# A second plain pair of chunks, and another order of units, in the two feed-forward stages of an encoder layer

## The reference

```python
x = layer_norm(ALPHA * x + 0.5 * swiglu(x, ffn1...), ...)
x = layer_norm(ALPHA * x + hybrid_mixer(x, ...), ...)
x = layer_norm(ALPHA * x + memory_cross_attention(x, mem, ...), ...)
x = layer_norm(ALPHA * x + 0.5 * swiglu(x, ffn2...), ...)

def swiglu(x, w_gate, w_up, w_down):      # 1024 -> 2816 -> 1024
    return (silu(x @ w_gate) * (x @ w_up)) @ w_down
```

## Time and profile before

| | us |
|---|---|
| median of three runs (1238.31 to 1239.45) | 1238.95 |
| the profiled execution, its own time | 1240.66 |
| its span, first to last instruction | 1238.9 |
| TensorE busy in the span | 1190.8 |
| VectorE, ScalarE, POOL busy | 940.2, 624.1, 257.3 |

### The profile page before, as it was taken

The page is one execution under the profiler, slowest core; times in us unless marked ns, Lnnn a source line. Parts: engine busy times, 40 slices in busy tenths (PEclk is TensorE's granted clock), DMA queues, the critical chain, the costliest instruction groups (busy, mean ns, idle before and its releaser), DMA issues.

```text
span 1238.9 us, 18583 instructions
## 1 busy us (share of the span) xinstructions
PE 1190.8 (96%) x7307; PEld 1067.7 (86%) x7307; DVE 940.2 (76%) x1221; ACT 624.1 (50%) x955; POOL 257.3 (21%) x208
## 2 busy tenths in 40 slices
PE   8699999999999999999999999999969999999996
PEld 7689999999989888878888888888969989898995
DVE  5778888888868767777764577555887898978786
ACT  3654545454536767567642225341365454545453
POOL 3232323232102200111010020001332233332301
PEclk9899999999999999999999999999989999999999
DMA  8866877777846414222273516213665778786841
GB/s 262 249 152 177 197 195 182 206 182 211 198 138 207 141 45 108 72 60 68 69 221 102 170 34 188 80 39 119 186 146 120 217 166 221 153 235 140 239 120 68
DMA packets 140646, 188.42 MB, mean 152 GB/s; under 512 B 6528, under 2 KB 106896, under 8 KB 139536
## 3 DMA queue, kind: packets, MB, share of 16 engines
q1 hardware_dynamic: 121104, 126.92, 32.9%
q0 software_dynamic: 19248, 60.30, 23.4%
q10 hardware_dynamic: 208, 0.01, 0.0%
HBM read 137.93 MB, written 7.34 MB: 117 GB/s over the span
## 4 chain that ended last, share of the span: by engine, by line
PE 80%; DVE 12%; issue 4%; ACT 3%; DMA 1%; SPq 0%; DVEq 0%; ACTq 0%
PE bank L1085 16%; PE bank L1004 11%; PE banks_scores L1085 11%; PE bank L1006 11%; PE bank L1005 11%; DVE ring_lo L2089 5%; PE bank L1011 5%; PE banks_scores L1011 3%; PE banks_scores L1004 2%; PE banks_scores L1005 2%; PE banks_scores L1006 2%; DVE x_sum L2179 2%; ACT ring_hi L1628 2%; DVE op_lo L2089 1%; PE bank L1355 1%
## 5 line engine op out<-in xcount | busy, mean ns | idle before, releaser
L2089 DVE TENSOR_TENSOR ring_lo<-raw,ring_hi 128x1024 fp32r<-128x1024 f32 x191 | 245.7, 1290 | 95.8 <-ACT ring_hi L1628 95.3
L1628 ACT ACTIVATE ring_hi<-raw 128x1024 fp32r<-128x1024 f32 x191 | 200.7, 1056 | 93.0 <-PE bank L1006 33.2
L1085 PE MATMUL bank<-xT_hi,ring_hi 128*128 128x256 f32 x480 | 137.3, 286 | 7.3 <-DVE hf L2170 5.0
L1085 PE MATMUL bank<-xT_hi,ring_lo 128*128 128x256 f32 x480 | 137.3, 286 | 0.0
L1085 PE MATMUL bank<-xT_lo,ring_hi 128*128 128x256 f32 x480 | 137.2, 286 | 0.0
L1004 PE MATMUL bank<-xT_hi,ring_hi 128*128 128x512 f32 (+1 forms) x360 | 136.6, 379 | 0.3 <-DVE gate L2746 0.3
L1006 PE MATMUL bank<-xT_hi,ring_lo 128*128 128x512 f32 (+1 forms) x360 | 134.5, 374 | 0.0
L1005 PE MATMUL bank<-xT_lo,ring_hi 128*128 128x512 f32 (+1 forms) x360 | 134.3, 373 | 0.0
L1085 PE MATMUL banks_scores<-x_s,ring_hi 128*128 128x256 f32 x640 | 117.4, 284 | 6.9 <-DVE ring_lo L2089 6.9
L1085 PEld LDWEIGHTS banks_scores<-x_s,ring_hi 128*128 128x128 f32 x640 | 100.6, 192 | 11.1 <-DVE ring_lo L2089 10.1
L1085 PEld LDWEIGHTS bank<-xT_hi,ring_hi 128*128 128x128 f32 x480 | 93.3, 194 | 9.4 <-issue 8.0
(11 more groups left out here) (421 smaller groups left out, 3164.4 us busy)
## 6 DMA issues: line engine op xcount, KB each, us to landing
raw<-in_ffn_w_gate SPq DMA_DIRECT2D x44, 512.0 KB, 4.0
raw<-in_ffn_w_up SPq DMA_DIRECT2D x44, 512.0 KB, 5.6
wd<-in_ffn_w_down SPq DMA_DIRECT2D x20, 1024.0 KB, 5.1
raw<-in_mix_w_in SPq DMA_DIRECT2D x34, 512.0 KB, 3.8
t<-in_ffn_w_down SPq DMA_DIRECT2D x20, 512.0 KB, 7.3
raw<-raw POOLq DMA_DIRECT2D x20, 512.0 KB, 4.7
raw<-gate_t POOLq DMA_DIRECT2D x20, 512.0 KB, 5.6
t<-wd POOLq DMA_DIRECT2D x10, 512.0 KB, 6.7
```

The source lines that it names most:

```text
L1085: mm = pe.matmul(dst, a[:, k, cols], b[:, k, :], start=fresh, stop=True, skip_group_check=True)
L1628: nc.scalar.activation(dst, src, copy).then_inc(unit_hi, 1)
L2089: nc.vector.tensor_tensor(dst, src, hi.bitcast(F32), ALU.subtract).then_inc(done, 1)
```

## The change

The plain units become eight, so that the first two pairs are plain and groups run from 2 to 10 (`FIRST` is 2). The two further chunks use banks 0 to 3 again: chunk 2 waits for `hidden(0)`, chunk 3 for `hidden(1)`. The x sums and their halves move behind the hidden rows of the plain chunks, and have the same order in both stages. The units of quad 0 move from group 1 and 2 to groups 2 and 3. In every group pair the down units 1 and 4, and 5 and 2, stand together behind product 5. At the end down unit 5 goes ahead of the first four end tiles and down unit 6 behind them, and tiles 4 and 7 change places; `end_low(1)` moves behind the first four tiles, `add_product` of unit 5 ahead of them. The buffer `squares_1` moves to where gate_t1 lay.

```diff
-PLAIN = 4
+PLAIN = 8
+FIRST = PLAIN // 4
...
-    order += G(1, 0, 1, 4, 3, 5) + D(0, 0) + G(1, 2, 6)
     for d in range(1, QUADS):
         a, b, done = 2 * d, 2 * d + 1, d - 1
-        order += G(a, 0, 1) + (D(done, 0) if d > 1 else [])
-        order += G(a, 4, 3) + D(done, 1) + G(a, 5) + D(done, 4) + G(a, 2, 6) + D(done, 3)
-        order += G(b, 0, 1, 4, 3) + D(done, 5) + G(b, 5) + D(done, 2) + G(b, 2, 6) + D(done, 6)
+        order += G(a, 0, 1) + D(done, 0) + G(a, 4, 3, 5) + D(done, 1, 4) + G(a, 2, 6) + D(done, 3)
+        order += G(b, 0, 1, 4, 3, 5) + D(done, 5, 2) + G(b, 2, 6) + D(done, 6)
     a, done = GROUPS, QUADS - 1
-    order += G(a, 0, 1) + D(done, 0) + G(a, 4, 3) + D(done, 1) + G(a, 5) + D(done, 4) + G(a, 2) + D(done, 3) + G(a, 6)
+    order += G(a, 0, 1) + D(done, 0) + G(a, 4, 3, 5) + D(done, 1, 4) + G(a, 2) + D(done, 3) + G(a, 6)
...
-TILE_ORDER = (0, 1, 2, 3, 5, 7, 4, 6)
+TILE_ORDER = (0, 1, 2, 3, 5, 4, 7, 6)
...
-                for m in range(2):
+                for m in range(PLAIN // 2):
...
             def weight_sums(f):
 
-                gate_sums(f, 2)
-                gate_sum_21(f, 2)
...
-            gate_sums(0, 1)
+            gate_sums(0, FIRST)
             pool.wait_ge(xt_lo, T_X1)
...
-            gate_sum_21(0, 1)
             down_sums_0(0)
+            gate_sum_21(0, FIRST)
             weight_sums(0)
...
-                def gate_up(side, n):
+                def gate_up(side, n, chunk):
                     for m in range(2):
                         ready(n + m)
+                        if m == 0 and chunk >= 2:
+                            pe.wait_ge(h_full, hidden_count(f, 0) + chunk - 1)
                         project(n + m, bank(2 * side + m))
...
                 first_units() if f == 0 else first_units_2()
+                for chunk in (2, 3):
+                    gate_up(chunk % 2, n0 + 2 * chunk, chunk)
                 for kind, g, q in SEQUENCE:
...
                     elif kind == "D":
+                        down_quad_product(g, q)
                         if (g, q) == (QUADS - 1, 5):
                             for j in TILE_ORDER[:4]:
                                 end_tile(j)
-                        down_quad_product(g, q)
-                        if (g, q) == (QUADS - 1, 5):
-                            for j in TILE_ORDER[4:6]:
-                                end_tile(j)
-                for j in TILE_ORDER[6:]:
+                for j in TILE_ORDER[4:]:
                     end_tile(j)
...
                 prep(n0 + 4)
-                x_high(3)
                 prep(n0 + 5)
-                x_high(4)
                 silu(0)
...
                 prep(n0 + 6)
-                scale_block(0)
+                x_high(3)
                 prep(n0 + 7)
-                scale_block(1)
-                if f == 0:
-                    x_high(2)
                 silu(1)
                 prep(n0 + 8)
+                x_high(4)
+                scale_block(0)
+                silu(2)
+                prep(n0 + 9)
+                scale_block(1)
+                prep(n0 + 10)
+                x_high(2)
+                part_high(0, 0)
+                silu(3)
+                prep(n0 + 11)
+                scale_block(2)
+                prep(n0 + 12)
+                scale_block(3)
...
+                    add_product(QUADS - 1, 5)
                     end_tile(0)
-                    end_low(1)
                     end_tile(1)
                     mean(0, end_mean)
                     end_tile(2)
                     end_tile(3)
                     mean(1, end_mean)
-                    add_product(QUADS - 1, 5)
+                    end_low(1)
                     first_block()
                     end_tile(5)
-                    end_tile(7)
                     gain(3, x, 1)
                     end_tile(4)
                     centre(2)
+                    end_tile(7)
                     end_tile(6)
...
                 split(n0 + 4)
-                x_first_sum()
                 split(n0 + 5)
-                x_second_sum()
                 hidden(0)
...
                 split(n0 + 6)
+                x_first_sum()
+                split(n0 + 7)
+                hidden(1)
+                x_second_sum()
+                split(n0 + 8)
                 x_low(4)
-                split(n0 + 7)
                 x_low(3)
-                if f == 0:
-                    x_fourth_sum()
-                hidden(1)
-                split(n0 + 8)
+                split(n0 + 9)
+                hidden(2)
+                x_fourth_sum()
+                split(n0 + 10)
+                x_low(2)
+                split(n0 + 11)
+                part_low(0, 0)
+                hidden(3)
+                split(n0 + 12)
                 x_third_sum()
...
                         elif q == 1:
                             part_sum_4(d)
                             if d == 0:
+                                x_low(5)
                                 part_low(0, 1)
...
                         elif q == 6 and d == QUADS - 1:
+                            end_low(0)
                             part_low(d, 6)
-                            end_low(0)
```

More of the change, by code:

```diff
@@ L178, in raw_tables @@
         keys = [(ffn_unit(f, "P", 0, j), ffn_unit(f, "P", 0, j)) for j in range(PLAIN)]
-        keys += [((f, g, b), ffn_unit(f, "G", g, q)) for g in range(1, GROUPS + 1) for b, q in BLOCKS.items()]
+        keys += [((f, g, b), ffn_unit(f, "G", g, q)) for g in range(FIRST, GROUPS + 1) for b, q in BLOCKS.items()]
         keys += [(ffn_unit(f, "L", 0, r), ffn_unit(f, "L", 0, r)) for r in range(2)]
@@ L375, in program @@
         gate = place("gate", [P, 2, SEQ], F32, z_gate)
-        squares_1 = place("squares_1", [P, 2, D], BF16, z_gate)
+        squares_1 = place("squares_1", [P, 2, D], BF16, z_q)
         c_hi = place("c_hi", [P, SEQ], BF16, z_p + 4096)
@@ L549, in group_no @@
         def group_no(f, g):
-            return GROUPS * f + g - 1
+            return (GROUPS + 1 - FIRST) * f + g - FIRST
         def hidden_count(f, g):
@@ L699, in ffn_units @@
                 for name in BLOCKS:
-                    block(1, name)
+                    block(FIRST, name)
                 if f == 0:
@@ L709, in ffn_units @@
                 down_rows(1, 0)
-                for name in BLOCKS:
-                    block(2, name)
                 for d in range(1, QUADS):
@@ L980, in _ @@
             pool.wait_ge(om_full, KC)
-            gate_sums(1, 1)
-            gate_sum_21(1, 1)
+            gate_sums(1, FIRST)
             down_sums_0(1)
+            gate_sum_21(1, FIRST)
             weight_sums(1)
@@ L1052, in corners_free @@
                     if q == 0:
[L1053 removed]
+                        pe.wait_ge(*((silu_done, hidden_count(f, g - 2) + 2) if g > FIRST + 1 else (h_full, hidden_count(f, 1) + 1)))
                     elif q == 1:
[L1055 removed]
+                        pe.wait_ge(*((corner, k - 2) if g > FIRST else (h_full, hidden_count(f, 1) + 2)))
                     elif q == 4:
                         pe.wait_ge(snap, k + 1)
[L1058 removed]
+                        pe.wait_ge(x_sum_lo, 4 * f + X_LOWS[q])
                     elif q == 3:
[L1060 removed]
+                        if g > FIRST:
                             pe.wait_ge(corner, k)
[L1062 removed]
+                        pe.wait_ge(x_sum_lo, 4 * f + X_LOWS[q])
                     elif q == 5:
                         pe.wait_ge(snap, k + 2)
[L1065 removed]
+                        pe.wait_ge(x_sum_lo, 4 * f + X_LOWS[q])
                     elif q == 2:
                         pe.wait_ge(corner, k + 2)
[L1068 removed]
+                        pe.wait_ge(x_sum_lo, 4 * f + X_LOWS[q])
                     elif q == 6:
@@ L1759, in ffn @@
                         silu_first(g)
-                    if g == 1 and kind == "G":
-                        if q in (1, 4):
-                            scale_block(2 + (q == 4))
-                        elif q == 0:
+                    if kind == "G" and g % 2 == 0:
+                        d = g // 2 - 1
+                        if (g, q) == (FIRST, 0):
+                            part_high(0, 1)
                             x_high(5)
-                            part_high(0, 0)
-                        elif q == 3 and f == 1:
-                            x_high(2)
-                        elif q == 6:
-                            part_high(0, 1)
-                    elif kind == "G" and g % 2 == 0:
-                        d = g // 2 - 1
-                        if q == 1:
+                        elif q == 1:
                             part_high(d, 4)
@@ L2368, in centre_first @@
                                                        op0=ALU.add, op1=ALU.mult).then_inc(gained, 1)
+                    add_product(QUADS - 1, 5)
                     end_tile(0)
-                    end_low(1)
                     end_tile(1)
                     mean(0, first_mean)
```

(16 more changed lines are left out.)

48 lines of the change are left out of this document (14 added, 34 removed).

## The result

The changed kernel takes 1201.08 us (median of 4 runs, 1200.91 to 1201.29) against 1239.2 for the kernel before beside it: a ratio of 0.9692, 95% interval 0.9675 to 0.9709. It is faster, as forecast, by 38.1 us; the forecast of 1198.7 is 2.4 us too low, and its range of 1195 to 1211 holds the time. The profiled execution took 1201.12 us, its span is 1199.2.

A forecast was written before the change was run, and what follows sets the result against it. TensorE, busy 96% of the span, was taken as the bound, with its few standing places. Savings of 15.2 + 12.6 + 8.2 + 4.3 = 40.3 us took the profiled 1240.66 to 1200.4, median forecast 1198.7, range 1195 to 1211.

The forecast's parts named there:

- Part 1: Both stage starts: keeping the second pair plain adds 3.7 us of TensorE work but removes standing, saving 15.2 and 12.6.
- start of stage 1: From the plain pair's end to group 2, 39.93 us becomes 24.77 if nothing stands: 15.2 saved.
- start of stage 2: From the plain pair's end to group 2, 37.41 us less 24.77: 12.6 saved.
- eight quad stands: TensorE's 1.02 us stand before product 2, eight times alike, goes whole: 8.2 us, other bound 0.
- nothing stands: Both starts: hidden rows, x sums and product 5's low half come in time, the last with 2.3 us to spare.
- Part 2: Per quad, two down units between the corner's copy and product 2 give the corner 5.5 us instead of 2.75; saves 8.2.
- Part 3, stage 1: End of stage 1: D5 ahead of the first four tiles, D6 earlier; the third memory-key unit's wait of 1.0 goes.
- Part 3, stage 2: Kernel's end: VectorE no longer stands for tile 4, with one more eviction ahead of the last; 1.7 us saved.
- The rival of the late low half: Product 5's low half lengthened by POOL's gate add: up to 1.5 us a stage, 1201.7 us; chance 0.15.
- quad stand: Rival: waits before product 2 stay because VectorE is too far behind; all eight give 1206.9 us; chance 0.12, whole or part.
- moved start wait: Rival: hidden rows late ahead of product 1 in both stages, 16.8 us, so 1215.5; chance 0.06.
- products 5 not held by the corner's copy: Denies the slower rival: ScalarE's corner copy outlasts product 3 in 18 groups; 1242 us if 5.3 behind product 4; chance 0.03.

The follow-up runs named there:

- e3: Kernel before, first x sum steps, their copies and low halves moved behind the first hidden rows, still one plain pair: 1236.26 us against 1238.66, ratio 0.9975.
- e2: Changed kernel with the first five x sum steps and their two high copies put back ahead of the first chunk's hidden rows: 1210.97 us.
- e4: Kernel before, TensorE's order kept, VectorE's split at D1 and D5 moved behind the corner subtraction: 1230.1 us against 1238.66, ratio 0.9927.
- e11: Changed kernel with the old order of D1, D5 and product 5, and VectorE's split behind the corner subtraction: 1200.43 us.
- e6: Changed kernel with the evictions of tiles 7 and 6 and two means ahead of the centring of block 2 on VectorE: 1198.26 us.

## Why the prediction was right, and where it was not

The terms, by the starts of units in the two traces. Product 4 of group 2 stands behind all that part 1 moves: 83.49 to 68.14 in stage 1. Product 2 of group 10 closes the quads: 340.01 to 320.08, so 19.93, of which 15.35 are the start's. Between the stages the shift is 23.31 (the wait at 846.28 is at 822.97). In stage 2 product 4 goes from 944.04 to 907.88 and product 2 of group 10 from 1200.55 to 1160.74, so 39.81; less 23.31 and 12.85, 3.65 are left for the quads, from which the new stand of 0.79 is to be taken out.

| term | forecast | measured |
|---|---|---|
| start of stage 1 | 15.2 | 15.35 |
| start of stage 2 | 12.6 | 36.16 - 23.31 = 12.85 |
| eight quad stands | 8.2 | 4.58 + 4.44 = 9.0 |
| new stand in stage 2 | 0 | -0.8 |
| end of stage 1 | 2.6 | 23.31 - 19.93 = 3.4 |
| end of stage 2 | 1.7 | 39.7 - 39.81 = -0.1 |
| sum | 40.3 | 39.7 |

- **Part 1** held in its sizes and its reason. (The table's last term is the span's gain, 39.7, less 39.81.) The plain units took 21.77 us for 22.02; nothing stood, the clock stayed at 1.00. The Trainium skill's 131 ns per matmul of 512 columns (TensorE: Matmul & The Clock Gate, Back-to-back issue gap) did not come: 96 steps in 21.77 us are 227 ns. Of the reads behind "nothing stands", the thinnest was the low half for product 5: it ended at 72.36, 1.54 ahead of product 5, and in stage 2 at 912.48, 1.16 ahead, where 2.3 were reckoned. e3 shows that the order of the sums without the plain pair would have given 2.4 of the 28 us; e2, that the plain pair without the place of the first sums keeps some 18, and loses 2.3 in the waits that were expected and, by its rows through the store of mem's halves, far more; for the change itself that store cost nothing, as put down.
- **Part 2** held: 1.02 forecast for each, 1.11 to 1.15 measured, as the product behind each wait also begins slower (0.47 for its first row, now 0.40). The working named the right thing ("it stands on VectorE behind a split") but then credited the longer cover; e4 and e11 show that the place in the queue is enough. It also read the split's 2.23 us as a split's length: 1.0 of it, as much as a stand, is GpSimd's addition across it.
- **Part 3, stage 1** was under-sized: 3.4 for 2.6. The old unit behind the wait of 0.98 also ran slower (from 377.18 to the next at 383.35, 6.17 us, where the new one takes 5.83) and the wait costs an issue step.
- **Part 3, stage 2 is the step that failed**: "What is late next is VectorE itself, with one more eviction ahead of the last: 1.2 + 0.6, I take 1.7". The gain began 0.61 earlier than product 2 of group 10 did (1226.27 to 1185.85, 40.42), as reckoned, although it stood 0.73 for ScalarE's block, whose factor GpSimd had late (0.94 for 0.19 before). From there to VectorE's end it is 10.19 us, 9.60 before (1226.27 to 1235.87), and not 1.2 less: the stand of 1.17 went, but the eviction more costs 0.6, and the centring, which now follows the gain so soon that GpSimd's bias addition has just begun, loses 1.23 more than before. The working counted VectorE's queue and TensorE's tiles, and not GpSimd, which the gain starts. A reading in it was wrong as well: tile 4 goes from the seventh place of eight to the sixth, so it ends one tile (1.36 us) sooner beside the wait, not two; this cost nothing, as its eviction at 1186.99 did not stand for it.
- **The rival of the late low half** had the right mechanism at the wrong instruction. Product 5 did not wait; the split for a later unit was hit instead, and the price was 0.8 in one stage, within the "up to 1.5 us a stage" (by the working's own numbers, 15.5 less a cover of 14.3, that bound is 1.2). The rule that stood beside it (the Trainium skill, SBUF — State Buffer, Who interferes with whom) names the tail's loss as well: the trace agrees with it at 915.33 and 1187.96, and in e6 also with its other half, that a VectorE instruction with one SBUF input is not concerned.
- **The other rivals** fell: no quad stand, no moved start wait, products 5 not held by the corner's copy.
- **The sum** is 0.6 above the measured 39.7 partly by luck: four terms gave 2.0 us more than forecast, and two gave 2.6 less.
- **From the spans to the median**: by its own time the profiled execution went from 1240.66 to 1201.12, 0.7 above the 1200.4 of the sum. The other 1.7 of the 2.4 us come from the last step, "It lies 1.7 above the median of the three runs", which I carried over whole. It belonged to that execution of the kernel before; the one of after lies 0.04 from its median.

## What to carry to other kernels

When a product waits for a small operation, look first at what stands ahead of that operation in its own engine's queue, and at what lengthens it: moving one split gave what a new order of TensorE's units gave. When a tail is shortened, list every engine that an operation in it releases; here the gain started a GpSimd addition under which the next VectorE operation could not run, and filling that time with operations that read PSUM took 1.55 us off the tail. Room for late work is a matter of cover and order together: the order alone gave 2.4 of 28 us, the cover without the place of the first sums some 18.

## What the runs showed of the hardware

A VectorE operation over 128x1024 with two SBUF operands that lay across the end of a GpSimd addition of two 128x1024 operands ended 1.08 to 1.09 us behind it (915.33, 1187.96, and 95.71 and 1229.64 before), however early it had begun; one over 128x512 ended 0.55 behind (at 85.54, the addition at 84.99). The reverse holds as well: where VectorE's operations followed each other closely, the same addition lasted 5.54 us in stage 1 and 6.99 in e6, for 2.89 at 914.78. The fourteen longest additions of all traces ended 2.34 to 2.36 us behind the start of the next VectorE operation that has an operand in PSUM (79.29 in stage 1), as if GpSimd got in only there. A GpSimd product of 128x1 lasted 0.94 us across a VectorE operation, for 0.19. Two programs that are alike up to that point, the changed kernel and e6, fell to different sides of this; the changed kernel did so to the same side twice.
